# Attention in a fused two-block kernel: the value products of a step move one step later, between the scores and the turns of later steps

## The chip, the cores and the metric

One core of a Trainium2 chip runs the whole program in one launch. The metric is the device time of a launch in microseconds (us), the median of the runs. TensorE (PE in the rows) does all matrix products, VectorE (DVE) and ScalarE (ACT) the elementwise work and the softmax, GpSimd (POOL) splits the weights, SyncE (SP) issues the loads.

## What is computed

Two transformer layers and then a recurrent block, on 512 tokens of width 1024. The change touches only the attention of the two layers. Each layer has three attentions: neighbourhood attention on a grid (NA, 4 heads), a latent attention with a compressed key (MLA, 4 heads of width 96), and grouped-query attention (GQA, 8 query heads on 2 key heads):

```python
def one_block(qi):
    s = jnp.einsum('bqkgd,bskd->bkgqs', qi, k, preferred_element_type=jnp.float32) * scale
    p = jax.nn.softmax(s, axis=-1)
    return jnp.einsum('bkgqs,bskd->bqkgd', p.astype(v.dtype), v)
...
merged = (jax.nn.sigmoid(ga) * (o_na @ w_br_na)
          + jax.nn.sigmoid(gb) * (o_mla @ w_br_mla)
          + jax.nn.sigmoid(gc) * (o_gqa @ w_br_gqa))
x = x + g_m * (merged @ w_out)
```

## The kernel before

Activations lie channel-major, 128 channels by 512 tokens to a tile. A weight product is split into three passes (high by high, high by low, low by high): lines L358, L359 and L360, one **dense step** of three passes for each 128 rows of weights. A product is a chain of such steps into one of two PSUM banks (`ACC`, 0 and 1, by the product's number), so product p can begin only when product p - 2 has been taken out of its bank (`claim`). `in`, `q`, `k`, `v` products are taken out by ACT (a copy); the gates `ga`, `gc`, `gb` by ACT (a tanh, L743); the branches `na`, `gqa`, `mla` by DVE (`post`, L1799 for `na`).

The attention of a layer is a pipeline of 32 steps written out by hand. Steps 0 to 7 are NA (only the even ones are active), 8 to 23 are GQA, 24 to 31 are MLA. An active step handles 128 queries of two heads (h = 0, 1) and is spread over the engines so:

- PE `scores(s)`: query by key into the bank pair `SC` (L1201 for NA, L1212 else). It waits until the probabilities of the step before have been read out of that bank (`probs_ready`), head by head.
- DVE `maxima(s)` (L1929, L1931), then ACT the exponentials in place (L788), then DVE `weights_of(s)` (L1946, L1949), which writes `prob`.
- PE `turn_probs(s)`, one step later: eight transposes of `prob` into the bank pair `PT` (L1222), and ACT copies them to `pT` (L774). In ACT's queue the copies of step s - 1 stand ahead of the exponentials of step s.
- PE `times_v(s)`: the value products, sixteen half-width matmuls from `pT` and the values (L1235 for NA, L1242 else) into bank `OB`; DVE `outputs(s)` (L1963, L1965) then splits the result into `oT`.

Around these, each step has a fixed number of dense steps (`fills`): 4 + 3 + 3 in NA, 3 + 2 + 1 in GQA (2 + 1 + 1 in its last), 5 + 3 + 4 in MLA. They are the products of the layer, in one fixed list. In GQA the list has pieces of different length: gate products of eight steps, branch products of two, and in steps 10, 12, 14 and 16 small products of one or two steps (`q`, `k`, `v`) right behind a branch. In step 14, for example, the six dense steps are the last two of gate ga2, the two of branch na2, then k2 and k3 of one step each; k3 needs the bank that na2 leaves.

DVE also has work between maxima and weights in some steps: rotations of queries (`rope`, `q_rope`, L1819 to L1824 and L1870 to L1875) in steps 8, 10, 11, 13, 15, 17 and 19. In layer 0 DVE does besides one modulation product (L1648) in each step, three in an MLA step.

The order on PE within step s before the change is: scores(s), turn_probs(s - 1), f1 dense steps, times_v(s - 1), extra sums and turns if the step has any, f2 and f3 dense steps.

Of the kernel before, what the change touches and what calls it, by code (L numbers as in the profile page):

```python
# [38 lines left out]
NA, GQA, MLA, STEPS_ATT = 0, 8, 24, 32  # L39
# [61 lines left out]
def fills(s):  # L101
    return (4, 3, 3) if s < GQA else (3, 2, 1) if s < MLA - 1 else (2, 1, 1) if s < MLA else (5, 3, 4)


def active(s):

    return s >= GQA or s % 2 == 0


def att(s):  # L110

    return s - 4 if s >= GQA else s // 2
# [250 lines left out]
def build(nc, x, c, weights, ada_b, vec1, rpb, vec2_in, vecx_in, tables1, out):  # L363
    dram_bias = nc.dram_tensor("bias_rows", (DEPTH * 4 * 15, NA_WIDE), F32, kind="Internal")
    dram_copies = nc.dram_tensor("bias_copies", (DEPTH, NA_COLS, BIAS_ROWS), F32, kind="Internal")
    with ExitStack() as ctx:
# [150 lines left out]
        def evacuated(eng, p):  # L517

            eng.wait_ge(bank_free[p.mod(2)], ((p - p.mod(2)).half() + C_BANK + 1).value())
# [471 lines left out]
        def _(pe):  # L991
# [112 lines left out]
            for l in range(DEPTH):  # L1104
# [78 lines left out]
                def scores(s):  # L1183
                    b = s % 4
                    if s == NA:
                        evacuated(pe, Count(PR + 4))
                        evacuated(pe, Count(PR + 5))
                    elif GQA <= s < MLA and b == 0:
                        pe.wait_ge(rope_ready, 5 * l + (s - GQA) // 4 + 2)
                    elif s >= MLA and b == 0:  # L1190
                        pe.wait_ge(mla_ready, 2 * l + (s - MLA) // 4 + 1)
                        for h in range(4):
                            evacuated(pe, Count(PR + PIDX["k", h]))
                    for i in range(2 if s < GQA else 0):
                        n = s % 4 + i
                        for h in range(2):
                            u, rows = 2 * (ATT * l + att(s)) + h, slice(64 * h, 64 * h + 64)
                            q = pj[rows, s // 4, n * P:(n + 1) * P]
                            k = pj[rows, 2 + s // 4, 8 * BAND_AT[n]:8 * BAND_AT[n] + 8 * BAND]
                            pe.wait_ge(probs_ready, u - 1) if u > 1 and i == 0 else None  # L1200
                            mm = MM(ps[:, SC + h, 256 * i:256 * i + 256], q, k, start=True, stop=True)  # L1201
                            if i:
                                mm.then_inc(scores_ready, 1)
                    for h in range(2 if s >= GQA else 0):
                        u, rows = 2 * (ATT * l + att(s)) + h, slice(64 * h, 64 * h + 64)
                        if s < MLA:
                            q, k = pj[rows, 10 + (s - GQA) // 4, b * P:(b + 1) * P], pj[rows, 14, :]
                        else:
                            head = 2 * ((s - MLA) // 4) + h
                            q, k = pj[0:96, head, b * P:(b + 1) * P], pj[0:96, 4 + head, :]  # L1210
                        pe.wait_ge(probs_ready, u - 1) if u > 1 else None
                        MM(ps[:, SC + h, :], q, k, start=True, stop=True).then_inc(scores_ready, 1)  # L1212

                def turn_probs(s):
                    for h in range(2):
                        u = 2 * (ATT * l + att(s)) + h
                        pe.wait_ge(probs_ready, u + 1)
                        pe.wait_ge(p_copied, u - 1) if u > 1 else None
                        if s in TURNED_BY:
                            pe.wait_ge(vt_copied, N_TURNS * l + TURNED_BY[s])  # L1220
                        for kb in range(4):
                            mm = nc.tensor.transpose(ps[:, PT + h, kb * P:(kb + 1) * P], prob[:, h, kb * P:(kb + 1) * P], ident[:])  # L1222
                        mm.then_inc(p_turned, 1)

                def times_v(s):
                    before = ATT * l + att(s)
                    if before:
                        pe.wait_ge(ot_used, before)
                    pe.wait_ge(p_copied, 2 * before + 2)
                    if s < GQA:  # L1230
                        v_of = vna[:, :, :] if s // 4 else vt[:, 0:2].rearrange("p t a n -> p (t a) n")
                        for i in range(2):
                            for kb in range(2):
                                for h in range(2):
                                    mm = MM(ps[64 * h:64 * h + 64, OB, i * P:i * P + P], v_of[:, 2 * (s % 4 + i) + kb, 64 * h:64 * h + 64],  # L1235
                                            pT[:, h, 2 * i + kb, :], start=(kb == 0), stop=(kb == 1))
                        mm.then_inc(pv_done, 1)
                        return
                    tile = 2 if s < MLA else (s - MLA) // 4
                    for kb in range(4):  # L1240
                        for h in range(2):
                            mm = MM(ps[64 * h:64 * h + 64, OB, 0:P], vt[:, tile, kb, 64 * h:64 * h + 64], pT[:, h, kb, :],  # L1242
                                    start=(kb == 0), stop=(kb == 3))
                    mm.then_inc(pv_done, 1)
# [3 lines left out]
                def fill(n):  # L1248
                    for _ in range(n):
                        next(work_left, None)  # L1250
# [13 lines left out]
                for s in range(STEPS_ATT):  # L1264
                    f1, f2, f3 = fills(s)
                    if active(s):
                        scores(s)
                    if s and active(s - 1):
                        turn_probs(s - 1)
                    fill(f1)  # L1270
                    if s and active(s - 1):
                        times_v(s - 1)
                    if s:
                        for p, _ in ENDS[s - 1]:
                            if PRODS[p][0] == "in" and PRODS[p][1] in NORMS:
                                sum_tile(PRODS[p][1])
                    for j in TURN_AT.get(s, ()):
                        turn(j)
                    fill(f2)
                    fill(f3)  # L1280
                turn_probs(STEPS_ATT - 1)
                fill(3)
                times_v(STEPS_ATT - 1)
# [334 lines left out]
        def _(dve):  # L1618
# [141 lines left out]
            for l in range(DEPTH):  # L1760
# [26 lines left out]
                def ended(p):  # L1787

                    dve.wait_ge(tile_used, TI + PRODS[p][3] + 1)
# [161 lines left out]
                def outputs(s):  # L1951
                    tile = s // 4 if s < GQA else 4 + (s - GQA) // 4 if s < MLA else 2 + (s - MLA) // 4
                    if s == GQA + 12:
                        ended(PIDX["v", 1])
                    dve.wait_ge(pv_done, ATT * l + att(s) + 1)
                    hi, lo = (oT[:, part, tile, (s % 4) * P:(s % 4 + 1) * P] for part in (0, 1))
                    src = ps[:, OB, 0:P]
                    if s < GQA:
                        at = NA_COLS * (s % 4)
                        hi, lo = (oT[:, part, tile, :].rearrange("p (r c) -> p r c", c=GRID)[:, :, at:at + 2 * NA_COLS]  # L1960
                                  .rearrange("p r (i c) -> p i r c", i=2) for part in (0, 1))
                        src = ps[:, OB, 0:2 * P].rearrange("p (i r c) -> p i r c", i=2, r=8)
                    v(V.tensor_copy(hi, src))  # L1963
                    v.sync()
                    V.tensor_tensor(lo, src, hi, ALU.subtract).then_inc(ot_used, 1)  # L1965

                for s in range(STEPS_ATT):
                    if active(s):
                        maxima(s)
                    for p, early in ENDS[s]:  # L1970
                        if early and PRODS[p][0] in GATE_OF:
                            post(p)
                    between(s)
                    if active(s):
                        weights_of(s)
                    if s and active(s - 1):
                        outputs(s - 1)
                    behind(s)
                    late = [p for p, early in ENDS[s] if not early and PRODS[p][0] in GATE_OF]
                    soon = [p for p in late if PRODS[p + 1][2] < KD]  # L1980
                    for p in soon:
                        post(p)
                    if l == 0:
                        rows_done = modulate(rows_done, DUE["step", s])
                    for p in late:
                        if p not in soon:
                            post(p)
                outputs(STEPS_ATT - 1)
                for p in range(MERGED, P_OUT):
                    if PRODS[p][0] in GATE_OF:  # L1990
# [583 lines left out]
```

## Time and profile before

| | us |
|---|---|
| median of 3 runs | 2866.44 |
| lowest and highest run | 2864.52 and 2867.47 |
| profiled execution | 2864.96 |
| its span, first to last instruction | 2863.2 |
| attention steps of layer 0 (first scores 70.6, last value products 369.7) | 299.1 |
| attention steps of layer 1 (first scores 877.7, last value products 1174.4) | 296.7 |

PE is busy for 98% of the span and its granted clock is 0.998 over it, so time is lost or won only where PE waits or where one of its passes takes longer than the next pass needs to follow. A row of a timeline gives the start, the duration, the engine, the line, the operation and its tiles. Matmuls overlap, so what counts on PE is the distance from the start of one row to the start of the next.

### The profile page before, as it was taken

How to read it: one execution, taken by the hardware profiler on the slowest of the kernel's cores; microseconds unless marked ns; L12 is line 12 of the kernel's file. 1: busy time of each engine (PE TensorE's matmuls, PEld its weight loads, DVE VectorE, ACT ScalarE, POOL GpSimd, SP SyncE). 2: the span in 40 equal slices, each digit the busy share in tenths (PEclk: the TensorE clock that was granted, in tenths of full speed). 3: DMA queues.
4: the chain of work that ended last, by engine and by line, in shares of the span. 5: the costliest groups of instructions: out<-in, count | busy, mean ns of one | idle time of the engine just before them, and what ended most of it. 6: DMA issues, size and time to landing. Idle time of an engine off the chain costs nothing.

```text
span 2863.2 us, 44335 instructions
## 1 busy us (share of the span) xinstructions
PE 2818.1 (98%) x18030; PEld 2239.2 (78%) x18030; DVE 1559.8 (54%) x2283; ACT 676.8 (24%) x1158; POOL 1657.7 (58%) x1332
## 2 busy tenths in 40 slices
PE   8999999999999999999999999999999999999998
PEld 6767787888877767878888777877787787788886
DVE  7888875555236664453333385665465556662342
ACT  4443212000023442120000034233323333310000
POOL 4435577787865334667677745344444434676774
PEclk9999999999999999999999999999999999999999
DMA  7334543444322112232223321112112211222221
GB/s 280 104 119 133 202 164 109 146 148 151 128 91 79 41 62 71 74 103 96 96 96 103 99 74 62 57 64 69 51 60 69 71 54 68 77 96 98 100 96 59
DMA packets 89588, 280.50 MB, mean 98 GB/s; under 512 B 12318, under 2 KB 23326, under 8 KB 89246
## 3 DMA queue, kind: packets, MB, share of 16 engines
q1 hardware_dynamic: 85904, 274.70, 28.4%
q10 hardware_dynamic: 3502, 3.26, 0.6%
q8 instruction: 127, 2.08, 0.3%
q14 instruction: 55, 0.45, 0.1%
HBM read 275.80 MB, written 2.62 MB: 97 GB/s over the span
## 4 chain that ended last, share of the span: by engine, by line
PE 91%; DVE 6%; issue 1%; ACT 1%; DMA 0%; SPq 0%; DVEq 0%; ACTq 0%
PE ps L358 25%; PE ps L360 24%; PE ps L359 24%; PE ps L1404 3%; PE ps L1212 2%; PE ps L1222 2%; PE ps L1242 2%; PE ps L1449 1%; DVE first_mod L1718 1%; PE ps L1037 1%; PE ps L1033 1%; PE ps L1034 1%; PE ps L1526 0%; DVE mg L1813 0%; PE ps L1368 0%
## 5 line engine op out<-in xcount | busy, mean ns | idle before, releaser
L592 POOL TENSOR_TENSOR wR<-raw,wR 128x512 fp32r<-128x512 f32 (+1 forms) x866 | 1198.3, 1403 | 68.7 <-ACT wR L649 31.7
L588 POOL CAST wR<-raw 128x1024 fp32r<-128x1024 f32 (+3 forms) x462 | 465.2, 1007 | 1105.2 <-PE ps L360 983.6
L358 PE MATMUL ps<-hR,wR 128*128 128x512 f32 x2224 | 901.5, 405 | 6.9 <-DVE hR L1739 6.9
L359 PE MATMUL ps<-hR,wR 128*128 128x512 f32 x2224 | 868.5, 390 | 0.0
L360 PE MATMUL ps<-hR,wR 128*128 128x512 f32 x2224 | 868.2, 390 | 0.0
L358 PEld LDWEIGHTS ps<-hR,wR 128*128 128x128 f32 x2224 | 418.0, 188 | 112.5 <-issue 21.0
L360 PEld LDWEIGHTS ps<-hR,wR 128*128 128x128 f32 x2224 | 418.0, 188 | 89.4
L359 PEld LDWEIGHTS ps<-hR,wR 128*128 128x128 f32 x2224 | 418.5, 188 | 81.7 <-issue 4.3
L1697 DVE SCALAR_TENSOR_TENSOR xT<-ps,lm,xT 128x512 f32<-128x512 f32 x32 | 24.0, 751 | 216.0 <-PE ps L360 215.9
L358 PE MATMUL ps<-act_f,wR 128*128 128x512 f32 x352 | 137.7, 391 | 0.0
L360 PE MATMUL ps<-act_f,wR 128*128 128x512 f32 x352 | 136.9, 389 | 0.0
L359 PE MATMUL ps<-act_f,wR 128*128 128x512 f32 x352 | 136.9, 389 | 0.0
L1648 DVE CUSTOM_DVE_ANT_0 raw<-raw,cs 128x1024 f32<-128x1024 f32 x80 | 127.8, 1614 | 7.4 <-DVE act_f L1675 4.9
L806 ACT ACTIVATE tg<-ps 128x512 f32<-128x512 f32 x44 | 26.4, 600 | 423.0 <-PE ps L360 421.2
L2011 DVE SCALAR_TENSOR_TENSOR work<-ps,work 128x512 f32<-128x512 f32 x44 | 30.4, 692 | 173.6 <-PE ps L360 173.5
L625 ACT ACTIVATE sq<-xT 128x512 f32<-128x512 f32 x48 | 30.2, 631 | 317.0 <-DVE xT L1697 202.6
L774 ACT ACTIVATE pT<-ps 128x512 f32<-128x512 f32 x112 | 60.9, 596 | 169.4 <-PE ps L1222 169.4
L358 PE MATMUL ps<-mlpR,wR 128*128 128x512 f32 x256 | 100.0, 391 | 0.0
L360 PE MATMUL ps<-mlpR,wR 128*128 128x512 f32 x256 | 99.6, 389 | 0.0
L359 PE MATMUL ps<-mlpR,wR 128*128 128x512 f32 x256 | 99.6, 389 | 0.0
L1929 DVE TENSOR_REDUCE top<-ps 128x1 f32<-128x512 f32 x96 | 65.8, 685 | 34.8 <-PE ps L1212 34.2
L2409 DVE TENSOR_TENSOR work<-ps,work 128x512 f32<-128x512 f32 x16 | 11.1, 692 | 133.6 <-PE ps L360 133.6
(394 smaller groups left out, 4189.0 us busy)
## 6 DMA issues: line engine op xcount, KB each, us to landing
raw<-in_weights_dram SPq DMA_DIRECT2D x468, 512.0 KB, 3.3
first_mod<-in_weights_dram SPq DMA_DIRECT2D x16, 512.0 KB, 10.3
raw<-in_weights_dram SPq DMA_DIRECT2D x50, 128.0 KB, 2.4
raw<-in_weights_dram SPq DMA_DIRECT2D x16, 256.0 KB, 2.8
raw<-in_weights_dram SPq DMA_DIRECT2D x8, 384.0 KB, 10.2
xT<-in_x_dram SPq DMA_DIRECT2D x1, 2048.0 KB, 9.3
rpb_wide<-bias_copies ACTq DMA_DIRECT2D x16, 128.0 KB, 4.3
out_dram<-xT SPq DMA_DIRECT2D x4, 512.0 KB, 2.6
```

Source lines behind the costliest of these rows:

```text
L358: mm(out, w_hi, r_hi, start=first, stop=False)
L359: mm(out, w_hi, r_lo, start=False, stop=False)
L360: return mm(out, w_lo, r_hi, start=False, stop=last)
L588: nc.gpsimd.tensor_copy(wR[:, u, 0, 0:cols], raw[:, r % RING, 0:cols]).then_inc(hi_done, 1)
L592: ins = nc.gpsimd.tensor_tensor(wR[:, u, 1, part], raw[:, r % RING, part], wR[:, u, 0, part], ALU.subtract)
L774: A(pT[:, h].rearrange("p a n -> p (a n)"), ps[:, PT + h, :], ACT.Copy).then_inc(p_copied, 1)
L1212: MM(ps[:, SC + h, :], q, k, start=True, stop=True).then_inc(scores_ready, 1)
L1222: mm = nc.tensor.transpose(ps[:, PT + h, kb * P:(kb + 1) * P], prob[:, h, kb * P:(kb + 1) * P], ident[:])
L1242: mm = MM(ps[64 * h:64 * h + 64, OB, 0:P], vt[:, tile, kb, 64 * h:64 * h + 64], pT[:, h, kb, :], start=(kb == 0), stop=(kb == 3))
L1404: return MM(ps[half_of(at_half), bank, col + 64 * cc:col + 64 * cc + 64], left[half_of(half), h, cc, :], right[half_of(half), h, cc, :], s ...
L1648: V.tensor_tensor_reduce(raw[:, r % RING, :], raw[:, r % RING, :], cs[:], 1.0, 0.0, ALU.mult, ALU.add, accum_out=mod[:, j:j + 1]).then_inc ...
L1929: v(V.tensor_reduce(top[:, h:h + 1], src, AX_X, ALU.max, negate=True))
```

## The change

A new function `valued(s)` names the steps whose value products are done in step s: step s - 2 instead of s - 1, with step 24 doing both 22 and 23 (23 at its old place, since the first GQA branch product needs it in the same step), and step 25 none. On PE they now stand between `scores(s)` and `turn_probs(s - 1)`. On DVE `outputs` follows the same list and stays behind `weights_of(s)`. The last two steps are closed by hand. Nothing is added or taken away: all engines have as many instructions as before.

```diff
+def valued(s):
+    return ([s - 2] if s > 1 and active(s - 2) and s != MLA + 1 else []) + ([s - 1] if s == MLA else [])
...
                     if active(s):
                         scores(s)
+                    for step in valued(s)[:1]:
+                        times_v(step)
                     if s and active(s - 1):
                         turn_probs(s - 1)
                     fill(f1)
-                    if s and active(s - 1):
-                        times_v(s - 1)
+                    for step in valued(s)[1:]:
+                        times_v(step)
...
+                times_v(STEPS_ATT - 2)
                 turn_probs(STEPS_ATT - 1)
...
                         weights_of(s)
-                    if s and active(s - 1):
-                        outputs(s - 1)
+                    for step in valued(s):
+                        outputs(step)
...
+                outputs(STEPS_ATT - 2)
                 outputs(STEPS_ATT - 1)
```

PE at the start of GQA step 14, before: the last dense pass of step 13, scores (L1212), turns (L1222), the first dense passes of the step.

```order
L360 MATMUL ps<-hR,wR 128x512
L1212 MATMUL ps<-pj 128x512 x2
L1222 MATMUL ps<-ident,prob 128x128 x8
L358 MATMUL ps<-hR,wR 128x512
L359 MATMUL ps<-hR,wR 128x512
```

After (line numbers below the new function are five to nine higher):

```order
L365 MATMUL ps<-hR,wR 128x512
L1217 MATMUL ps<-pj 128x512 x2
L1247 MATMUL ps<-pT,vt 64x128 x8
L1227 MATMUL ps<-ident,prob 128x128 x8
L363 MATMUL ps<-hR,wR 128x512
```

The value products, now those of step 12, stand ahead of the turns of step 13.

PE in the middle of the same step, before: the first step of branch na2 (`oT`), the value products of step 13 (L1242), the second step of na2, the first pass of k2 (64 wide).

```order
L358 MATMUL ps<-oT,wR 128x512
L359 MATMUL ps<-oT,wR 128x512
L360 MATMUL ps<-oT,wR 128x512
L1242 MATMUL ps<-pT,vt 64x128 x8
L358 MATMUL ps<-oT,wR 128x512
L359 MATMUL ps<-oT,wR 128x512
L360 MATMUL ps<-oT,wR 128x512
L358 MATMUL ps<-oT,wR 64x512
```

After:

```order
L363 MATMUL ps<-oT,wR 128x512
L364 MATMUL ps<-oT,wR 128x512
L365 MATMUL ps<-oT,wR 128x512
L363 MATMUL ps<-oT,wR 128x512
L364 MATMUL ps<-oT,wR 128x512
L365 MATMUL ps<-oT,wR 128x512
L363 MATMUL ps<-oT,wR 64x512
```

Nothing stands between the two steps of na2 any more; the eighteen dense passes of the step follow one another.

DVE in NA step 3 of layer 0, before: the reading of a modulation product's sum, the reciprocal and product of the latent key's norm (L1669, L1840), the outputs of step 2 (L1963, L1965), the split of the latent key (L1673, L1675).

```order
L1648 ISA mod 128x1
L1669 RECIPROCAL work<-work 128x512
L1840 SCALAR_TENSOR_TENSOR work<-pj,lv,work 128x512
L1963 CAST oT<-ps 128x2x8x16
L1965 TENSOR_TENSOR oT<-ps,oT 128x2x8x16
L1673 CAST oT<-work 128x512
L1675 TENSOR_TENSOR oT<-work,oT 128x512
```

After:

```order
L1656 ISA mod 128x1
L1677 RECIPROCAL work<-work 128x512
L1848 SCALAR_TENSOR_TENSOR work<-pj,lv,work 128x512
L1681 CAST oT<-work 128x512
L1683 TENSOR_TENSOR oT<-work,oT 128x512
```

Step 3 has no outputs; those of step 0, which stood in step 1, now stand at the end of step 2, behind its probabilities. So between the probabilities of step 2 and the maxima of step 4 DVE has one pair of outputs before and after.

## Rows read from the trace of the kernel before

**Rows 1.** The page: the chain that ended last, by engine.

```profile
PE 91%; DVE 6%; issue 1%; ACT 1%; DMA 0%; SPq 0%; DVEq 0%; ACTq 0%
```

**Rows 2.** Timeline of PE, GQA step 22, layer 0: start us, duration us, engine, line, tiles.

```profile
257.08 1.13 PE L1212 MATMUL ps<-pj 64*128 64x512 f32 x4
258.14 1.09 PE L1222 MATMUL ps<-ident,prob 128*128 128x128 f32 x8
...
260.69 0.39 PE L359 MATMUL ps<-hR,wR 128*128 128x512 f32 x1
260.92 0.39 PE L360 MATMUL ps<-hR,wR 128*128 128x512 f32 x1
261.24 1.09 PE L1242 MATMUL ps<-pT,vt 128*64 128x128 f32 x16
262.26 0.50 PE L358 MATMUL ps<-hR,wR 128*128 128x512 f32 x1
262.60 0.40 PE L359 MATMUL ps<-hR,wR 128*128 128x512 f32 x1
...
264.52 0.70 PE L1212 MATMUL ps<-pj 64*128 64x512 f32 x2
```

**Rows 3.** Timeline of PE, MLA step 25, layer 0, to the next scores.

```profile
282.56 1.88 PE L1212 MATMUL ps<-pj 96*128 96x512 f32 x4
284.28 1.04 PE L1222 MATMUL ps<-ident,prob 128*128 128x128 f32 x8
...
288.67 1.09 PE L1242 MATMUL ps<-pT,vt 128*64 128x128 f32 x16
289.69 0.50 PE L358 MATMUL ps<-hR,wR 128*128 128x512 f32 x1
...
294.58 0.59 PE L1212 MATMUL ps<-pj 96*128 96x512 f32 x1
```

**Rows 4.** Timeline of all engines, GQA step 14, layer 0 (small products).

```profile
194.46 1.35 PE L1212 MATMUL ps<-pj 64*128 64x512 f32 x4
...
195.74 1.09 PE L1222 MATMUL ps<-ident,prob 128*128 128x128 f32 x8
...
196.43 1.09 ACT L774 ACTIVATE pT<-ps 128x512 f32<-128x512 f32 x2 [5.06 <-PE ps L1222]
...
197.40 0.76 ACT L788 ACTIVATE ps<-ps,nmax,rq 128x512 f32<-128x512 f32 x1
...
198.85 1.09 PE L1242 MATMUL ps<-pT,vt 128*64 128x128 f32 x16
198.91 0.61 ACT L743 ACTIVATE sq<-ps 128x512 f32<-128x512 f32 x1
...
199.37 0.75 DVE L1949 TENSOR_SCALAR prob<-ps,rinv 128x512 f32<-128x512 f32 x1
...
200.03 0.28 DVE L1963 CAST oT<-ps 128x128 fp32r<-128x128 f32 x1
...
200.95 0.69 DVE L1799 SCALAR_TENSOR_TENSOR mgacc<-sq,ps 128x512 f32<-128x512 f32 x1 [0.31 <-PE ps L360]
...
201.79 0.42 PE L358 MATMUL ps<-oT,wR 128*64 128x512 f32 x1 [0.25 <-DVE mgacc L1799]
...
202.59 1.13 PE L1212 MATMUL ps<-pj 64*128 64x512 f32 x4
```

**Rows 5.** Timeline of all engines, GQA step 15, layer 0 (rotation on DVE).

```profile
203.65 1.09 PE L1222 MATMUL ps<-ident,prob 128*128 128x128 f32 x8
...
209.74 0.75 DVE L1949 TENSOR_SCALAR prob<-ps,rinv 128x512 f32<-128x512 f32 x1
...
211.60 0.44 PE L1222 MATMUL ps<-ident,prob 128*128 128x128 f32 x2
```

**Rows 6.** Timeline of all engines, NA steps 4 and 5, layer 0.

```profile
114.02 0.42 DVE L1923 CUSTOM_DVE_ANT_0 ps<-ps,bias 128x256 f32<-128x256 f32 x1
...
117.84 0.41 PE L1222 MATMUL ps<-ident,prob 128*128 128x128 f32 x2 [0.95 <-ACT vt L712]
```

## Prediction, written before the changed kernel ran

> **What bounds the kernel now.** I read the page first: the chain that ended last runs for 91% of the span on PE and for 6% on DVE [rows 1]. So the change can act in two ways only: PE needs less time to get from one kind of matmul to the next, or PE waits more or less for DVE and ACT. Then I read PE's timeline over one undisturbed GQA step [rows 2] and one MLA step [rows 3], as distances between starts. Two dense passes follow each other in 0.23 us (260.69 to 260.92). Around the value products the distances are longer: 0.32 from the last dense pass to the first value matmul, 1.02 from there to the next dense pass, and 0.34 instead of 0.23 to the one after [rows 2]. Last I read all engines over a step in which PE waits for DVE, of which there are two kinds [rows 4, 5].
>
> **What the edit saves on PE itself.** Work is the same; what goes is the time of turning PE from dense passes to value products and back.
>
> GQA. Before, a free step lasts 264.52 - 257.08 = 7.44 us: scores to turns 1.06, turns to value products 3.10, value products to dense passes 1.02, dense passes to the next scores 2.26 [rows 2]. After, the order is scores, value products, turns, dense. Scores to their successor I keep at 1.06 (they leave the same 64-row shape, and the trace has no step from scores to half-width matmuls); value products to their successor stay 1.02; turns and eighteen dense passes then take 3.10 + 2.26, less the 0.09 (0.32 - 0.23) into and the 0.11 (0.34 - 0.23) out of the value products: 5.16. Sum 1.06 + 1.02 + 5.16 = 7.24, so 0.20 saved. The bounds: if scores to value products cost one more such turn, 0.09 of it is lost; if value products go over into turns for nothing, up to 0.15 more is won (a pass of 512 columns takes 0.43 in the scores of rows 3, so that eight pairs of 128 columns 0.87, and 1.02 is 0.15 more) [rows 2, 3].
>
> MLA. Before 294.58 - 282.56 = 12.02 us [rows 3]. The scores use 96 rows and go over into the turns with no loss: 284.28 - 282.56 = 1.72, four passes of 0.43 each. After, 1.72 + 0.09 into the value products, 1.02, and 4.39 + 4.89 less the same 0.09 and 0.11, plus 0.05 for the first turn: 11.96. So 0.06 saved.
>
> NA. The scores there are a block of their own, as the value products are; joining them saves one way in and out, which I price like GQA, 0.20.
>
> In each layer there are 4 NA value products, 14 in GQA that move in front of turns, and 8 in MLA: 4 x 0.20 + 14 x 0.20 + 8 x 0.06 = 4.1 us, in two layers 8.2 us. This is what would come if PE never waited.
>
> The Trainium skill, TensorEngine Tiling (Array Packing), Key Properties, says that changing the tiling mode drains the array. By that rule a GQA step goes from four changes (whole, rows, whole, columns, whole) to three, but an MLA step, whose scores are not row-tiled, has two before and two after and wins nothing; the sum would be 1 us smaller. No row here shows the joint of scores and value products, so the trace cannot decide that yet.
>
> **What is given back.** The value products took 1.02 us out of the middle of the dense passes; now they push the turns back by 1.02 us from the scores. ACT copies the turned probabilities of step s - 1 before it takes the exponentials of step s: the turns start at 195.74, the copies at 196.43, the exponentials at 197.40, 1.66 behind the turns [rows 4]. So the exponentials, the probabilities, the outputs and the posts behind them on DVE all come 1.02 later after the scores, while the dense passes of the step end sooner. Four kinds of step follow.
>
> (a) Steps with small products, 12, 14 and 16. In step 14 DVE's post of na2 frees the bank of k3. Before, na2 ends late since the value products stand in it: DVE is free at 200.64 and waits 0.31 for PE, posts at 200.95, k3 starts at 201.79 (0.84 later) and the next scores at 202.59, 1.64 behind the post [rows 4]. From the end of the scores (195.74, when the turns start) that is 6.85. After, the dense passes no longer hold DVE up, but DVE holds up PE: turns at 1.02, exponentials at 2.68, outputs 2.63 later (200.03 - 197.40), DVE free another 0.61 later (200.64), at 5.92, scores 1.64 later at 7.56. So such a step gets longer by 0.71 rather than shorter by 0.20. Three steps in two layers: 4.3 us. The bounds: 0.4 if the outputs and the post close up faster than these rows, 1.0 if the tanh of the gate on ACT adds its own wait.
>
> The Trainium skill, Perfetto Trace Analysis, Optimizing Tensor Performance (Matmuls), asks that independent groups rotate through PSUM banks so that one is read out while the next is filled. It speaks against the change where two banks carry products of one or two steps; the 0.71 above is from rows alone.
>
> (b) Steps with rotations on DVE, 10, 11, 13, 15, 17 and 19. In step 15 the second head's probabilities start at 209.74, behind the rotation, and the next scores are held by them: the turns come at 211.60, 7.95 behind those at 203.65, where a free step has 7.44 [rows 5]. DVE starts this chain from the scores, ACT is long done when the rotation ends, so the chain keeps its 7.95 and the saved 0.20 becomes a longer wait. Change 0. Steps 8 and 9 I take with them: step 8 takes over the value products of step 6, which covers its wait for a rotation, and step 9, whose exponentials already come late, gets longer; I take the two as equal.
>
> (c) Free GQA steps. Steps 20, 21, 22 save 0.1 to 0.2 each. In step 18 the gate ga5 needs the tanh of ga4, which stands behind the later exponentials: 1.66 + 1.51 + 0.61 + 0.15 = 3.93 behind the turns, where PE arrives at 3.69 (3.10 - 0.09 + one dense step of 0.68); the saving is gone [rows 2, 4]. Step 23 has two dense steps less and is held by its probabilities by 0.1. Together -0.45 a layer.
>
> (d) NA and MLA have slack: -0.6 (three NA steps; the fourth is in step 8) and -0.45 a layer.
>
> Per layer -0.6 + 0 + 2.1 - 0.45 - 0.45 = +0.6, in two layers +1.2 us.
>
> One wait goes besides, in layer 0 only. The turns of step 4 stand 0.95 idle, at 117.84, for a chain on DVE that begins with the scores of step 2 and has DVE at work without a break up to the maxima at 114.02 [rows 6]. Value products of step 0 no longer stand ahead of the scores of step 2, so that chain starts 1.2 earlier (0.09 + 1.02 + 0.11); PE itself comes 0.4 earlier (two savings of 0.20); the wait shrinks by 0.8. DVE's pair of outputs in the chain is exchanged, not removed.
>
> Sum: +1.2 - 0.8 = +0.4 us on the profiled execution of 2864.96, which is 1.5 under the median of the runs; on the median 2866.44 + 0.4 = 2866.8, rounded to 2867. Queues off this path: SP and POOL have the same instructions in the same order and follow PE's freeing of tiles, which shifts by less than 2 us; the clock is granted in full before and I expect no change.
>
> **The rivals.** *The savings show in full.* If the small products do not wait longer (DVE's posts come early enough), the 8.2 us and the 0.8 come through: 2866.4 - 9.0 = 2857.4, 0.3% faster. For it: DVE no longer waits for value products before its outputs. Against it: the wait at k3 exists before, and every step of the chain to it is queued on one engine. If the posts come only half as late, 2862. Chance 0.17.
>
> *The chain through ACT becomes the pace of every GQA step.* From scores to scores it takes after the change 1.06 + 1.02 + 1.66, then 1.97 to the second head's probabilities (199.37 - 197.40), then 0.81 to the scores they release (211.60 - 1.05 - 209.74): 6.5 us against a step of 7.24 [rows 2, 4, 5]. The margin is 0.7 us. If maxima, copies or exponentials come later by more than that, each free step waits too: at 1.2 us late five free steps lose 0.5 and three small-product steps 1.2 in each layer, 12 us in all, 2879; at 0.9 late 7 us, 2874. For it: in layer 0 a modulation product stands ahead of the maxima. Against it: the margin is larger than any delay of the maxima in these rows. Chance 0.11, at 2874.
>
> **How the numbers follow.** The bounds of the forecast: turns of PE between 0.1 and 0.35 a GQA step move it by -4 and +3; small-product steps between 0.4 and 1.0 by 2 either way; noise of a median about 1.5. So 2862 to 2871 for the forecast, with 0.72. To hold 8 in 10 I reach down halfway to the first rival: 2860 to 2871. A measurement of this kernel tells 0.2%, 5.7 us, from no change. Faster by more than that 0.17, same 0.72, slower 0.11.
>
> **What would show it.** Right: free GQA steps of 7.24 us and MLA steps of 11.96; 1.02 from value products to turns; steps 12, 14 and 16 at about 8.5 from the end of one scores to the end of the next, with k1, k3 and v1 waiting some 1.3 us for DVE's L1807 (the post's new line); exponentials at 3.7 behind the scores; rotation steps unchanged at 7.9; the wait of DVE's outputs for the value products gone. Wrong: free steps under 7.1 or over 7.4, small-product steps that do not get longer, or waits for probabilities in steps 21 and 22.

## The result and the profile after

The changed kernel takes 2871.76 us (median of 20 runs, 2866.71 to 2874.20), the kernel before 2866.09 on the same chip (20 runs). The ratio is 1.0018, with a 95% interval of 1.0012 to 1.0024: 5.7 us longer, just under the 0.2% that the prediction counts as no change, and 0.8 us above the upper end of its range. The forecast of +0.4 us is refuted: the interval is +3.4 to +6.9 us.

The profiled execution of after lasts 2872.69 us (span 2870.9, mean granted clock 0.996; before 2864.96, 2863.2 and 0.998). The chain that ended last has moved from PE to DVE by one or two hundredths [rows 1]:

```profile
PE 89%; DVE 7%; ACT 1%; issue 1%; DMA 0%; SPq 0%; DVEq 0%; ACTq 0%
```

What the edit saves on PE itself came as forecast. This is PE's timeline of after over GQA step 22 (start us, duration, engine, line, tiles); it answers to [rows 2]:

```profile
258.59 1.13 PE L1217 MATMUL ps<-pj 64*128 64x512 f32 x4
259.64 1.09 PE L1247 MATMUL ps<-pT,vt 128*64 128x128 f32 x16
260.67 1.09 PE L1227 MATMUL ps<-ident,prob 128*128 128x128 f32 x8
261.52 0.47 PE L363 MATMUL ps<-hR,wR 128*128 128x512 f32 x1
261.83 0.39 PE L364 MATMUL ps<-hR,wR 128*128 128x512 f32 x1
...
265.81 0.70 PE L1217 MATMUL ps<-pj 64*128 64x512 f32 x2
```

Scores to value products 1.05, value products to turns 1.03, turns to the next scores 5.14: 7.22, against 7.44 before and 7.24 forecast. The eighteen dense passes are one stretch.

The small products of step 14 wait through the chain that was forecast, though k3 waits 0.83 us for the post and not some 1.3. All engines of after, to be read beside [rows 4]:

```profile
194.94 1.57 PE L1217 MATMUL ps<-pj 64*128 64x512 f32 x4
...
196.44 1.09 PE L1247 MATMUL ps<-pT,vt 128*64 128x128 f32 x16
...
197.47 1.09 PE L1227 MATMUL ps<-ident,prob 128*128 128x128 f32 x8
...
199.13 0.75 ACT L793 ACTIVATE ps<-ps,nmax,rq 128x512 f32<-128x512 f32 x1
...
201.09 0.75 DVE L1957 TENSOR_SCALAR prob<-ps,rinv 128x512 f32<-128x512 f32 x1
...
201.76 0.28 DVE L1971 CAST oT<-ps 128x128 fp32r<-128x128 f32 x1
...
202.28 0.68 DVE L1807 SCALAR_TENSOR_TENSOR mgacc<-sq,ps 128x512 f32<-128x512 f32 x1
...
203.11 0.42 PE L363 MATMUL ps<-oT,wR 128*64 128x512 f32 x1 [0.83 <-DVE mgacc L1807]
...
203.92 1.13 PE L1217 MATMUL ps<-pj 64*128 64x512 f32 x4
```

From the end of the scores (196.44, where the value products start) the turns stand at 1.03, the exponentials at 2.69, the outputs at 5.32, the post at 5.84, the next scores at 7.48; forecast were 1.02, 2.68, 5.31, 5.92 and 7.56.

The places that were not forecast show when all steps are laid side by side. The table gives the distance from the end of one step's scores to the end of the next step's, read from PE's timelines (the end is the start of what follows the scores: turns in before, value products in after), as after minus before in us:

| steps | layer 0 | layer 1 | both | forecast |
|---|---|---|---|---|
| NA 0 to 6 (value products of step 0 set off) | -0.78 | -0.66 | -1.4 | -2.0 |
| 8, 9, 10 | +0.62, -0.46, +1.02 | the same | +2.4 | 0 |
| 11 | +0.48 | -0.22 | +0.3 | 0 |
| 12 to 17 | +0.60, 0, +0.63, -0.31, +0.60, +0.15 | +0.64, -0.28, +0.64, 0, +0.62, -0.01 | +3.3 | +4.3 |
| 18 to 23 | -0.6 | -0.55 | -1.1 | -0.9 |
| 24, 25 | +1.60, -1.15 | +1.60, -1.15 | +0.9 | -0.2 |
| 26 to 31 | -0.30 | -0.31 | -0.6 | -0.7 |

The sum, added before rounding, is +3.6 us where the forecast has +0.5 by the same lines. The other 4 us of the span are not in the attention: they are two stretches behind it in which the clock was granted at half. Busy times of PE, weight load, DVE, ACT and POOL, then granted clock, DMA share and GB/s, in two stretches of after (start:end, length first):

```profile
1677.40:1684.10 6.70, 6.70 (x15) 4.88 (x16) 4.46 (x11) 5.03 (x8) 3.89 (x4) 0.50 0.21 78
1738.80:1742.10 3.30, 3.30 (x21) 3.09 (x20) 0.00 (x0) 1.42 (x3) 0.00 (x0) 0.50 0.00 0
```

0.50 is 1.2 GHz, 1.00 is 2.4 GHz. Ahead of the first PE had been idle for 1.55 us; the passes behind it follow each other in 0.43 us instead of 0.23:

```profile
1677.36 0.76 PE L363 MATMUL ps<-xaR,wR 64*128 64x512 f32 x1 [1.55 <-DVE vB L2145]
1677.92 0.62 PE L364 MATMUL ps<-xaR,wR 64*128 64x512 f32 x1
1678.35 0.62 PE L365 MATMUL ps<-xaR,wR 64*128 64x512 f32 x1
```

Before has nearly the same idle time and the full clock behind it in the profiled execution:

```profile
1673.62 0.46 PE L358 MATMUL ps<-xaR,wR 64*128 64x512 f32 x1 [1.53 <-DVE vB L2136]
```

Of the kernels below, two have one run each that lies far outside (2986.30 us in after_filled, 15888.19 in outs_small); without it their medians move by less than 0.1 us. So two questions go to the chip: which chains make steps 10, 12, 14, 16 and 24 longer, and whether the low clock belongs to the change.

### The profile page after: what moved, and what is told of

Same layout as the page of the kernel before. It is cut to its first block, busy times and chain, and to the rows that moved or that the text cites. A ratio compares the mean times of both kernels' runs of the same rounds, so it can differ in the third digit from the quotient of the medians.

```text
span 2870.9 us, 44333 instructions
## 1 busy us (share of the span) xinstructions
PE 2816.5 (98%) x18030; PEld 2243.9 (78%) x18030; DVE 1559.0 (54%) x2283; ACT 677.5 (24%) x1158; POOL 1658.1 (58%) x1332
## 4 chain that ended last, share of the span: by engine, by line
PE 89%; DVE 7%; ACT 1%; issue 1%; DMA 0%; SPq 0%; DVEq 0%; ACTq 0%
PE ps L363 25%; PE ps L364 24%; PE ps L365 24%; PE ps L1412 3%; PE ps L1217 2%; PE ps L1227 2%; PE ps L1247 2%; PE ps L1457 1%; DVE first_mod L1726 1%; DVE work L1691 1%; PE ps L1042 1%; DVE hR L1698 1%; PE ps L1534 0%; DVE mg L1821 0%; PE ps L1462 0%
## 6 DMA issues: line engine op xcount, KB each, us to landing
first_mod<-in_weights_dram SPq DMA_DIRECT2D x16, 512.0 KB, 10.5
```

## The experiments

Each kernel was run 11 times beside before (2865.9 to 2866.1 us); after_b and after_c are single profiled executions of after. After's median of 2871.76 was taken in a session of its own, so a difference "less than after" compares two sessions, in which before had the same median within 0.2 us. "Attention" is the sum of the step distances over both layers against before, the value products that after defers set off; what lies between the two layers varies by up to 0.6 and is left out. "Theory" and "rival" are those of the expectation printed above each result.

**A shift alone.** Is half the clock behind the attention a matter of the later start?

```diff
+                    if l == 1 and u == 4:
+                        warm(17)
                     bank = claim(Count(PR + P_DOWN + u))
```

> Before, with 17 extra products (ones times ones into a bank that is free) in the middle of the down products of layer 1, where PE runs without a break: 34 passes of 0.112 us, 3.8 us more work, all else later by that. It asks whether a shift alone brings the two stretches at half the clock that the profile of after has behind the attention (6.83 us and 3.41 us, about 3.9 us of time). Theory 1 (the shift brings them): the time is 3.8 plus 2 to 4 us above before, 2872 to 2874, mean granted clock 0.996. Theory 2 (they come from the changed attention itself, or from chance): 2866.1 + 3.8 = 2869.9, clock 0.998.

Measured: 2870.09 us, ratio 1.0013 (1.0004 to 1.0022), +4.1 us where the added work was estimated at 3.8, fastest 2868.47. So theory 2 holds. One stretch of 3.4 us at half the clock stands at 1679.1 in its profile. Runs of before also lie in groups, at 2864.5, 2866.0, 2867.5 and 2869.0, with a mean granted clock of 0.998, 0.997, 0.997 and 0.996, though its one profile has no such stretch. A shift alone does not bring 2 to 4 us.

**Outputs ahead of the probabilities in every step.**

```diff
+                    for step in valued(s)[:1]:
+                        outputs(step)
                     if active(s):
                         weights_of(s)
-                    for step in valued(s):
+                    for step in valued(s)[len(valued(s)[:1]):]:
                         outputs(step)
```

> After, with one pair exchanged on DVE: the outputs of the value products that stand ahead of the turns are read before the probabilities of the step are made, not behind them; nothing else moves. Theory (DVE's chain from exponentials over probabilities and outputs to the post is what holds the small products): in steps 12, 14 and 16 the post comes 0.6 us earlier (0.28 + 0.31 of the two output operations), the distance from one end of scores to the next falls from 8.53 to 7.93, in two layers 3.6 us; in step 24 the second value products no longer wait 0.5 for the outputs of the first, 1.0 us in two layers; step 9 may lose up to 0.3 each, since the NA outputs now stand ahead of its predecessor's probabilities. Sum -4.0 to -4.6 on the time of after. Rival (the small products wait for the tanh of the gate on ACT or for the end of na on PE): the post comes no earlier, steps 12, 14 and 16 keep 8.5, total change within 1 us (step 24 alone). Step 10 keeps its 9.96 in both.

Measured: 2871.16 us, ratio 1.0017 (1.0007 to 1.0026), no gain against after. Steps 12, 14 and 16 fell from 8.53 to 8.01 and step 24 from 13.63 to 13.11, as the theory has it. But steps 13, 15, 17 and 19 rose from 7.65 (step 17 of layer 0: 7.89) to 8.17 and step 10 from 9.96 to 10.5: there the probabilities, not the post, end the chain, and the outputs now stand ahead of them. My expectation forgot the steps in which PE waits for the probabilities themselves. Its profile also has 3.4 us at half the clock behind step 10 in both layers (at 170.7 and 979.6).

**Outputs ahead only where a post or a second value product is waited for** (the loop above runs only `if s in (12, 14, 16, 24)`).

> After, with the outputs of the value products ahead of the probabilities on DVE in steps 12, 14, 16 and 24 alone; in the rotation steps they stay behind. In the run where they stood ahead in all steps, steps 12, 14 and 16 fell from 8.53 to 8.01 and steps 13, 15, 17 and 19 rose from 7.65 to 8.17: what the post won the next probabilities lost. Theory (each of the two chains on DVE is paid for by the operations ahead of its own end): 8.01 in steps 12, 14 and 16, 7.65 in the rotation steps, step 24 at 13.1 instead of 13.6: 8 x 0.52 = 4.2 us less than after. Rival (the post that comes earlier only moves the wait to the next step's probabilities): the rotation steps rise again to about 8.1, and step 24's 1.0 is all that is left.

Measured: 2865.36 us, ratio 1.0002 (0.9993 to 1.0012): 6.4 us less than after, of which 4.8 are in the attention: 4.1 in steps 12, 14, 16 and 24, as the theory has it (4.2), and 0.75 in step 4 of layer 0, which varies between executions (below). Steps 12, 14 and 16 take 8.00 to 8.07, the rotation steps keep 7.63 to 7.67 (step 17 of layer 0: 7.89), step 24 takes 13.14. DVE in step 12 of this kernel:

```profile
181.71 0.28 DVE L1971 CAST oT<-ps 128x128 fp32r<-128x128 f32 x1
...
184.18 0.75 DVE L1957 TENSOR_SCALAR prob<-ps,rinv 128x512 f32<-128x512 f32 x1
184.85 0.68 DVE L1807 SCALAR_TENSOR_TENSOR mgacc<-sq,ps 128x512 f32<-128x512 f32 x1
```

The outputs are in the time in which DVE waited for exponentials, and the post follows the probabilities at once. That settles the small products: DVE's order from exponentials to post is what holds PE there.

**Step 10: the rotation ahead of the post.** DVE of before, of after and of the new kernel in step 10 of layer 0 (L1799 and L1807 are the post of na0, the shuffle begins the rotation, the last line is the second head's probabilities):

```profile
165.31 0.69 DVE L1799 SCALAR_TENSOR_TENSOR mgacc<-sq,ps 128x512 f32<-128x512 f32 x1 [0.72 <-PE ps L360]
...
165.93 0.73 DVE L1819 STREAM_SHUFFLE work<-pj 128x512 f32<-128x512 f32 x1
...
169.80 0.75 DVE L1949 TENSOR_SCALAR prob<-ps,rinv 128x512 f32<-128x512 f32 x1
```

```profile
164.92 0.69 DVE L1807 SCALAR_TENSOR_TENSOR mgacc<-sq,ps 128x512 f32<-128x512 f32 x1 [1.89 <-PE ps L365]
...
165.53 0.73 DVE L1827 STREAM_SHUFFLE work<-pj 128x512 f32<-128x512 f32 x1
...
169.41 0.75 DVE L1957 TENSOR_SCALAR prob<-ps,rinv 128x512 f32<-128x512 f32 x1
```

```profile
163.06 0.74 DVE L1827 STREAM_SHUFFLE work<-pj 128x512 f32<-128x512 f32 x1
...
165.90 0.69 DVE L1807 SCALAR_TENSOR_TENSOR mgacc<-sq,ps 128x512 f32<-128x512 f32 x1
...
167.56 0.75 DVE L1957 TENSOR_SCALAR prob<-ps,rinv 128x512 f32<-128x512 f32 x1
```

From the post to the probabilities it takes 4.49 us in before and in after: the chain is the same, and it starts from the post, hence from the end of na0, not from the scores. In after na0 comes 1.02 later behind the scores, DVE waits 1.89 instead of 0.72, and step 10 gets longer by 1.02.

```diff
+                    if s == 10:
+                        between(s)
                     for p, early in ENDS[s]:
                         if early and PRODS[p][0] in GATE_OF:
                             post(p)
-                    between(s)
+                    if s != 10:
+                        between(s)
```

> After, with step 10's rotation on DVE ahead of the post of na0, which in after waits 1.89 us for the end of na0 on PE while the rotation (2.8 us) stands behind it. The rotated tile has been ready since before step 9. Theory (step 10 got longer because the rotation's start, and with it the probabilities, hang on na0, which comes 1.02 later with the turns): DVE uses the 1.89 for the rotation, the probabilities come 1.9 earlier, step 10 falls from 9.96 to about 8.1 to 8.5, in both layers together -3 to -4 us against after. Rival (step 10 is held by the exponentials, which are themselves 1.02 later): the probabilities come at most 0.5 earlier, -1 us in all.

Measured: 2863.63 us, ratio 0.9993 (0.9984 to 1.0002), 8 us less than after. Step 10 falls from 9.96 to 8.03 and 7.40, the attention by 4.8 us. PE in layer 0, scores of step 11, in before, in after and then here:

```profile
169.75 1.98 PE L1212 MATMUL ps<-pj 64*128 64x512 f32 x4 [0.58 <-DVE prob L1949]
```

```profile
169.36 1.98 PE L1217 MATMUL ps<-pj 64*128 64x512 f32 x4 [1.78 <-DVE prob L1957]
```

```profile
168.27 1.22 PE L1217 MATMUL ps<-pj 64*128 64x512 f32 x4
```

The wait of 1.78 us is gone. The time fell by 3 us more than the attention, and its profile shows the full clock from 47 us to 2853 us.

**Does PE's wait in step 10 cost clock?** The same wait is filled with products that nobody needs; the attention stays as it is.

```diff
+                    if s == 11:
+                        for _ in range(7):
+                            MM(ps[:, SUM, 0:P], ones[:], ones[:], start=True, stop=True)
                     if active(s):
                         scores(s)
```

> After, with 7 extra products (14 passes of 0.112 us, 1.57 us) ahead of the scores of step 11, where PE waits 1.86 us for probabilities; they write a bank that nobody uses there. They end before the probabilities do, so the attention stays as long as in after, within 0.3 us. The median of after stands 5.0 us above its fastest run, that of before 1.5, and the kernel without this wait (rotation first) 1.2; the profile of the kernel with outputs first everywhere shows half the clock at 170.7 and at 979.6, right behind this wait. Theory (PE's long wait in step 10 draws stretches at half the clock in a part of the executions): the median falls by 2 to 3 us to 2869 or so, the fastest runs stay at 2867 to 2868. Rival (the stretches fall by chance, and the rotation-first kernel was merely shorter): median 2871 to 2872 as after.

Measured: 2868.91 us, 2.85 less than after, ratio to before 1.0012 (1.0002 to 1.0021), fastest 2866.97 as in after (2866.71). Step 10 keeps its length (9.98). Seven of its 11 runs are under 2869.1 us, of after's 20 runs four, and the granted clock of its runs, without the far one, is 0.997 in the mean where after has 0.996. The two 95% intervals against before overlap, so the 2.85 is a size with much room, not a measured cost.

> After unchanged, for a second profile. Theory on the clock (waits of PE in steps 10 and 11 draw it down in some executions): one or more stretches at half the clock within steps 9 to 13 of a layer. Rival (chance at the start of block 2): none in the attention, one or two near 1677 and 1738.

> After unchanged, for a third profile, with the same two expectations. The step lengths are expected as in the first profile to 0.05 us, but for the turns of NA step 4 in layer 0, which came 0.8 earlier in five of six other profiles with the same order there (step 4 at 19.2 to 19.5 instead of 20.21).

Measured: 2872.18 and 2871.51 us. Both have a stretch at half the clock right behind the wait in layer 1, at 977.6 and 976.8, 6.83 us long each, and one of 3.41 near 1680. The same two stretches of layer 1 in after's first profile, in the second (after_b) and in the filled kernel (columns as above: the last three are granted clock, DMA share, GB/s):

```profile
967.00:977.00 10.00, 8.66 (x49) 5.44 (x47) 6.82 (x15) 4.52 (x11) 3.08 (x5) 1.00 0.16 61
977.60:984.40 6.80, 6.80 (x42) 4.75 (x43) 6.52 (x16) 2.61 (x6) 2.26 (x2) 1.00 0.07 19
```

```profile
967.00:977.00 10.00, 8.23 (x47) 5.35 (x47) 6.80 (x15) 4.31 (x9) 3.71 (x6) 1.00 0.19 61
977.60:984.40 6.80, 6.80 (x30) 4.77 (x30) 4.84 (x11) 1.51 (x3) 1.54 (x2) 0.50 0.09 19
```

```profile
967.00:977.00 10.00, 9.78 (x61) 6.97 (x60) 6.81 (x15) 4.19 (x9) 3.73 (x6) 1.00 0.18 59
977.60:984.40 6.80, 6.80 (x45) 5.14 (x44) 6.52 (x16) 2.61 (x6) 1.43 (x2) 1.00 0.07 19
```

In the second profile of after, the value products and turns behind that wait take nearly twice as long (1.91 us from one to the other, 1.03 at the full clock):

```profile
976.72 2.93 PE L1217 MATMUL ps<-pj 64*128 64x512 f32 x4 [1.77 <-DVE prob L1957]
979.58 1.97 PE L1247 MATMUL ps<-pT,vt 128*64 128x128 f32 x16
981.49 1.97 PE L1227 MATMUL ps<-ident,prob 128*128 128x128 f32 x8
```

In the filled kernel the extra products stand in the wait, and what follows runs at full speed:

```profile
974.66 1.72 PE L1273 MATMUL ps<-ones 128*128 128x128 f32 x14
976.61 1.98 PE L1217 MATMUL ps<-pj 64*128 64x512 f32 x4 [0.23 <-DVE prob L1960]
978.52 1.09 PE L1247 MATMUL ps<-pT,vt 128*64 128x128 f32 x16
```

The stretch costs 3.2 us in steps 10 and 11 of layer 1 (10.92 + 9.50 against 9.96 + 7.25). Five profiled executions have this wait unfilled, 1.77 to 1.79 us long and 2.30 with outputs first everywhere. Three of them show half the clock behind it: the second and third of after in layer 1, outputs first in both layers, so four of ten such waits. The other eight, with 0.67 us of idle time or less at this place, have no low stretch between 60 us and the end of the attention. In which execution it comes is not predicted by anything seen here. That the wait draws it rests on this count and on the run times of the filled kernel together; one filled profile would not show it, since two unfilled ones have none either.

**Only parts of the change.** Only NA deferred (`LATE = (0, 2, 4, 6)`, all other value products as in before):

> Only the four NA value products move ahead of the next scores' turns; GQA and MLA stay as before. Theory (NA is all gain): NA steps -0.15 to -0.19 each as in the profile of after, the fourth fills the wait of 0.4 at the scores of step 9, so about -1.0 to -1.1 a layer and -2.0 to -2.2 us against before in two layers, granted clock as before. Rival (the outputs of step 6 now delay the probabilities of steps 8 and 9): half of it is given back in steps 8 to 10, -1.0. Second rival (any change of the attention's timing brings the low clock behind it): the time does not fall although the attention is shorter, with a lower granted clock in the run.

Measured: 2863.99 us, ratio 0.9993 (0.9984 to 1.0002). The attention is 3.6 us shorter: NA steps 0.15 to 0.2 each, step 8 with the value products of step 6 at 8.19, step 9 unchanged at 7.44, and the turns of step 4 in layer 0 come 1.1 earlier. Its profile has two stretches of 3.4 us at half the clock at 1671.7 and 1729.8, where the profiled execution of before has none; that may be why the time falls by 1.9 only. The interval leaves no change possible.

NA, the value products of steps 19 to 22 and MLA, outputs ahead of the probabilities:

> NA, GQA from the value products of step 19 on, and MLA are moved, GQA steps 8 to 18 stay as before, and the moved outputs stand ahead of the probabilities on DVE. Theory (only steps in which DVE is not in the chain gain): NA -1.0 a layer, four free GQA products -0.2 each, MLA -0.4, no wait at the second value products of step 24: -2.2 a layer at most, -4.4 us against before, 2861.7. Rival (step 20, now without value products, is held by its probabilities, and step 24 keeps a wait of 0.5): -0.6 to -1.0 less a layer, about 2863.5. Rival on the clock (a shorter attention draws a lower granted clock later): the attention shorter by 4 us, the total by less than 2.

Measured: 2860.28 us, ratio 0.9981 (0.9972 to 0.9990), 5.6 us less than before, attention -5.3. Free steps 7.22, step 24 at 13.11, step 20 at 7.09. The steps in which DVE ends no chain gain; the theory's -4.4 was too small because of the turns of step 4.

The same with step 10's rotation first:

> The kernel with NA, the free GQA steps and MLA moved (2860.3 us), with the rotation of step 10 ahead of the post of na0 as well. There the post waits 0.72 us for na0 in step 10 (as in before). Theory: 0.7 a layer less, -1.4, 2858.9. Rival (step 10 in this order is held by PE, not by the rotation): no change, 2860.3.

Measured: 2859.64 us, ratio 0.9978 (0.9969 to 0.9987). Step 10 falls by 0.54 in each layer (8.94 to 8.40), 0.1 is given back in step 11 of both; the attention is 0.8 shorter, half of the theory. The medians differ by 0.6, which is inside their intervals.

**Everything moved, both edits of DVE's order.**

> After with both edits: outputs ahead of the probabilities in steps 12, 14, 16 and 24, and the rotation of step 10 ahead of the post of na0. Theory (the two are independent places): the sum of the two, -7 to -8 us in the attention against after, so that the attention is 3.5 to 4.5 us shorter than in before and the time 2862 to 2864 by the fraction of runs with low-clock stretches. Rival (an earlier step 10 only leads into a longer wait in steps 11 and 12, which DVE holds anyway): not more than -5.

Measured: 2858.26 us, ratio 0.9974 (0.9965 to 0.9983): 7.8 us less than before and 13.5 less than after. The attention is 6.2 us shorter than before's and 9.8 shorter than in after's first profile; step 10 takes 8.02 and 7.40, steps 12, 14 and 16 8.00 to 8.07. The two edits add up. This version beats both kernels, and its time is near the first rival's 2857.4. But 2.5 of the 6.2 us are in step 10, which is now shorter than in before (8.95), so the gain is not the moved value products alone. What before itself would gain from the rotation ahead of the post was not run; in the kernel just above, whose step 10 is that of before, it was 0.8.

## Why the prediction was off, point by point

**The savings on PE: right.** 7.22 for 7.24 in free GQA steps, 11.96 for 11.96 in MLA steps, 0.15 to 0.19 for 0.20 in NA. The Trainium skill, TensorEngine Tiling (Array Packing), Key Properties, has the array drained at each change of tiling mode; by counting changes MLA would have won nothing. The rows speak against counting: MLA won 0.06 a step, GQA 0.22. Behind the value products the first dense pass took 0.11 us longer than between dense passes (0.34 against 0.23), while the turns in MLA take 0.85 behind them and 0.79 behind the scores, 0.06 more. So that joint is not as dear as one with dense passes.

**(a) Small products: right in mechanism and nearly in size.** +0.62 for +0.71 in steps 12, 14 and 16. The difference is the post: 0.52 behind the outputs, not 0.61. The post does not wait for the tanh, which ACT starts at 200.64 and ends at 201.25 in step 14, 1.0 ahead of it.

**(b) Rotation steps: wrong for step 10, near for 13, 15, 17 and 19.** In the attention this is the term that the sum had most wrong. The sentence that failed is "DVE starts this chain from the scores". In step 10 a post stands ahead of the rotation on DVE, so the chain starts from the end of a dense product that itself moved by 1.02. I had read one rotation step [rows 5] and carried it over to all; the order of DVE in step 10 shows the post. Steps 8 and 9 ("I take the two as equal") gave +0.16, so the three cost +1.18 a layer, +2.4 us in all, where the forecast has 0. Steps 13, 15, 17 and 19 gave -0.4 over both layers for 0. The 7.95 of rows 5 was not the length of the chain in general: other such steps of before take 7.64 to 7.91, and in step 15 one rotation product was longer, before and then after:

```profile
206.35 0.97 DVE L1872 TENSOR_TENSOR work<-work,tabm 32x512 f32<-32x512 f32 x1
```

```profile
207.67 0.68 DVE L1880 TENSOR_TENSOR work<-work,tabm 32x512 f32<-32x512 f32 x1
```

Step 15 fell to 7.64; a chain that "keeps its 7.95" was not seen, and why that product took 0.97 stays open.

**(c) Free steps: right.** -1.1 for -0.9, step 18 at +0.1 for 0.

**(d) NA and MLA: one place missed.** The term "-0.45 a layer" has no wait in it. Step 24 now holds two value products, and both write one bank. The second waits for the outputs of the first, which stand behind the probabilities on DVE. PE and DVE of after:

```profile
279.43 1.09 PE L1247 MATMUL ps<-pT,vt 128*64 128x128 f32 x16 [0.43 <-DVE oT L1973]
```

```profile
278.10 0.75 DVE L1957 TENSOR_SCALAR prob<-ps,rinv 128x512 f32<-128x512 f32 x1
278.77 0.28 DVE L1971 CAST oT<-ps 128x128 fp32r<-128x128 f32 x1
279.08 0.29 DVE L1973 TENSOR_TENSOR oT<-ps,oT 128x128 fp32r<-128x128 f32 x1
```

Steps 24 and 25 give +0.45 a layer where -0.12 was forecast. With the outputs ahead, 0.5 of it went.

**The turns of step 4 in layer 0: right, but not in the execution shown.** They came 0.28 earlier in step distance in the first profile of after (20.21 against 20.50), and 1.1 in the second and third (19.38 and 19.36); the forecast is 0.8 and the saving of 0.20. In nine of the ten other profiles with NA moved the step takes 19.2 to 19.5, in one 20.24 (the rotation-first kernel, with a copy of 1.40 in the same place). The chain on DVE lost 0.7 in one copy. After's first profile, then the second:

```profile
108.19 1.50 POOL L593 CAST wR<-raw 128x1024 fp32r<-128x1024 f32 x1 [2.30 <-DMA raw<-in_weights_dram]
...
108.83 1.14 DVE L1681 CAST oT<-work 128x512 fp32r<-128x512 f32 x1
```

```profile
108.91 0.43 DVE L1681 CAST oT<-work 128x512 fp32r<-128x512 f32 x1
...
109.12 1.11 POOL L593 CAST wR<-raw 128x1024 fp32r<-128x1024 f32 x1 [3.16 <-DMA raw<-in_weights_dram]
```

The copy takes 1.14 where POOL's cast had begun before it and 0.43 where it had not. That one causes the other was not tested. In the three kernels with all these outputs ahead of the probabilities the copy takes 1.23 and step 4 is early all the same, with a copy that starts over 1 us sooner.

**The clock: the sentence "I expect no change" failed.** The attention of a typical execution of after is 2.7 us longer (the filled kernel's profile, with the early turns of step 4, counted over everything from the first scores of layer 0 to the last value products of layer 1), and the fastest run of after is 2.2 above before's. Filling PE's wait took 2.85 us from the median. 2.7 + 2.85 is 5.6 of the 5.7 measured; that the two meet so closely is luck, given the intervals. So about half of the loss is in the attention's steps, where 8 to 17 and 24 lose more than the others win, and about half is clock lost behind PE's wait in step 10. The first profile did not show the second half where it belongs; its own two stretches lie in block 2, where eleven of thirteen profiles, those of mended and of before with the shift among them, have at least one.

**The rivals.** The ACT chain sets no pace, though the time lies nearer to its 2874 than to the forecast: steps 21 and 22 take 7.22. Full savings did not come by themselves; with DVE's order changed in five steps the kernel is 7.8 us faster than before, in part by step 10. None of the signs of being wrong that were named came: free steps take 7.22, the small products got longer, steps 21 and 22 show no wait. The loss lay in step 10, in step 24 and in the clock, for which no sign was set.

## What to carry to other kernels

When a block is moved on one engine, list for every step what ends the chain on the engine that reads its results, and do it step by step: a post, a rotation or a second write to one bank can stand at the head of it, and one step read closely does not speak for the others. Reorder the other engine's queue together with the move: what was ready early goes into its waits, what is waited for goes ahead. A wait of PE of nearly 2 us in the middle of dense work had a price beyond its length here; look at the granted clock behind such a wait, in more than one execution.

## What the runs showed of the hardware

Waits of PE of 1.5 to 2.3 us between stretches of dense passes were followed by stretches of 3.4 or 6.8 us at 1.2 GHz in some executions and by none in others, for the same kernel and the same wait. Behind 1.53 us in the profiled execution of before there was none; behind 1.78 us in after there was one in layer 1 in two of three profiles, and in layer 0 in none of three. The stretch of 6.8 us in layer 1 cost 3.0 and 3.2 us, and the times of before lie in groups about 1.5 us apart, which is more than most edits here are worth. With products into an unused bank in the wait, the filled kernel's profile kept the full clock there, and step 10 was 0.02 us longer.
